# One decoder layer step on one core: last weight piece of each expert block in two halves, sample norm on ScalarE and GpSimd

## The reference

```python
logits = xt @ router_w + router_b            # 32 experts, top 4 of each token
# slots sorted by expert and padded into blocks of rows
def expert(args):
    xb, e = args
    gu = xb @ w_gu[e] + b_gu[e]              # (rows, 1024) @ (1024, 2048)
    gate, up = split(gu); gate = min(gate, 7); up = clip(up, -7, 7)
    act = (up + 1.0) * gate * sigmoid(1.702 * gate)
    return act @ w_down[e] + b_down[e]       # (rows, 1024) @ (1024, 1024)
x = layer_norm(ALPHA * h + moe, ln2_g, ln2_b)
```

## Time and profile before

| what | us |
|---|---|
| median of three runs | 1507.08 |
| the profiled execution, device time | 1507.74 |
| its span in the trace | 1506.0 |
| last weight piece needed by TensorE | 1488.2 |
| last VectorE operation starts | about 1502.7 |

### The profile page before, as it was taken

One profiled execution on the slowest core, in us unless ns is written; L12 is line 12 of the kernel. 1 busy time (PEld: TensorE's weight loads), 2 busy tenths in 40 slices (PEclk: granted clock), 3 DMA queues, 4 the chain that ended last, 5 costly groups with the idle time before them and its releaser, 6 DMA issues.

```text
span 1506.0 us, 21874 instructions
## 1 busy us (share of the span) xinstructions
PE 1466.5 (97%) x8606; PEld 733.3 (49%) x8606; DVE 446.8 (30%) x918; ACT 344.6 (23%) x863; POOL 107.3 (7%) x95
## 2 busy tenths in 40 slices
PE   9999999999999999999999999999999999999997
PEld 7777776566777764333333333333333333333332
DVE  3653777867410137201101111111111101101113
ACT  1224215631110023211212112122112111211213
POOL 1002231010502401000000000000000000000000
PEclk9999999999999999999999999999999999999999
DMA  6346697546269777999999999999999999999996
GB/s 214 112 168 176 214 292 228 184 153 197 93 213 297 289 278 281 421 418 429 427 427 428 429 429 429 427 429 427 429 428 429 428 429 429 428 429 428 430 427 262
DMA packets 110574, 507.75 MB, mean 337 GB/s; under 512 B 12548, under 2 KB 49012, under 8 KB 85844
## 3 DMA queue, kind: packets, MB, share of 16 engines
q1 hardware_dynamic: 103840, 499.64, 83.0%
q10 hardware_dynamic: 6676, 7.29, 1.7%
HBM read 491.19 MB, written 15.72 MB: 337 GB/s over the span
## 4 chain that ended last, share of the span: by engine, by line
PE 67%; DMA 21%; DVE 3%; ACT 1%; issue 1%; DVEq 0%; SPq 0%; ACTq 0%
DMA wGU<-in_w_gu 21%; PE ps L2483 16%; PE ps L1944 12%; PE ps L2488 8%; PE ps L2251 4%; PE ps L2424 4%; PE ps L1960 3%; PE ps L2471 3%; PE ps L2475 3%; PE ps L2268 2%; PE ps L2389 2%; PE ps L2281 2%; PE ps L2405 1%; DVE up L1837 1%; DVE up L1836 1%; PE ps L2026 1%
## 5 line engine op out<-in xcount | busy, mean ns | idle before, releaser
L2483 PE MATMUL ps<-wGU,xe 128*64 128x512 f32 x1536 | 343.7, 595 | 15.6 <-DMA wGU<-in_w_gu 15.6
L2488 PE MATMUL ps<-wD,aT 128*64 128x512 f32 x1024 | 226.8, 595 | 0.0
L2483 PEld LDWEIGHTS ps<-wGU,xe 128*64 128x64 f32 x1536 | 108.5, 137 | 238.0 <-issue 211.3
L1944 PE MATMUL ps<-xT,ring 128*128 128x288 f32 (+1 forms) x848 | 180.7, 410 | 2.2 <-PEq L200 0.7
L1833 DVE TENSOR_SCALAR sg<-sg 128x512 f32<-128x512 f32 x32 | 13.7, 427 | 558.3 <-ACT sg L1276 558.3
L1944 PEld LDWEIGHTS ps<-xT,ring 128*128 128x128 f32 (+1 forms) x848 | 126.5, 172 | 46.3 <-issue 4.4
L2488 PEld LDWEIGHTS ps<-wD,aT 128*64 128x64 f32 x1024 | 71.4, 137 | 133.0 <-issue 126.2
L1276 ACT ACTIVATE sg<-ps 128x512 f32<-128x512 f32 x32 | 19.1, 598 | 487.3 <-PE ps L2471 487.3
L1225 ACT ACTIVATE xe<-ps,lnT 128x64 f32<-128x64 f32 x262 | 81.4, 422 | 1.2 <-PE ps L2398 1.2
L402 PE MATMUL ps<-xT,ring 128*128 128x288 f32 x320 | 78.1, 407 | 0.0
L1292 ACT COPY ysb<-ps 64x512 f32<-64x512 f32 x64 | 37.1, 580 | 155.3 <-PE ps L2488 154.5
(11 more groups left out here) (487 smaller groups left out, 1418.9 us busy)
## 6 DMA issues: line engine op xcount, KB each, us to landing
wGU<-in_w_gu SPq DMA_DIRECT2D x128, 2048.0 KB, 34.9
wD<-in_w_down SPq DMA_DIRECT2D x64, 2048.0 KB, 36.1
ring<-in_w_in SPq DMA_DIRECT2D x21, 2048.0 KB, 8.9
out<-hst SPq DMA_DIRECT2D x8, 1024.0 KB, 6.0
ringS<-in_ssd_proj SPq DMA_DIRECT2D x4, 2048.0 KB, 8.9
wbuf<-prompt_A_rows ACTq DMA_DIRECT2D x16, 384.0 KB, 4.3
out<-Sb SPq DMA_DIRECT2D x2, 2048.0 KB
ring<-in_hg_proj SPq DMA_DIRECT2D x2, 2048.0 KB, 9.2
```

The source lines that it names most:

```text
L1944: last = m.matmul(ps[h, b, 0:T], ring[c % 2][:, k, n * P + h.start:n * P + h.stop], xT[:, k, :], start=(k == 0), stop=(k == KD - 1))
L2483: last = m.matmul(ps[half[h], bank, :], xe[:, f, hx, :], wgu[n][:, k, col + CW * h:col + CW * h + CW], start=(i == 0 and k == 0), stop=False)
L2488: last = m.matmul(ps[half[h], B_Y, :], aT[:, k, i - 4, :], wdn[n][:, k, CW * h:CW * h + CW], start=False, stop=(i == 5 and k == 3))
```

## The change

Pieces 0 to 3 stay as they are. Piece 4 stays one transfer of 2 MB, but each partition now gets rows 2p and 2p+1 of each half of 256 rows: two runs of 8 KB. Piece 5 becomes two transfers of 1 MB, 256 rows each, with a semaphore of its own for the first half; TensorE waits for the first half before k = 0 and for the second before k = 2. The transposes of `up` take columns two apart in two halves, to match. In the tail the norm of the samples leaves VectorE: it only multiplies mean and 1/sigma (128 x 1), ScalarE makes x/sigma - mean/sigma in one operation, GpSimd multiplies by the weight and adds the bias, and ScalarE issues the output transfer. Some semaphores are merged to make room (`q_cb` into `q_A`, `h_ot` into `h_nt`, `t_gb` into `t_vt`); the merged waits are for the same events.

```diff
-                    rows = 256 if i < 4 else 512
-                    sp.dma_start(dst[:], src[0, bass.ds(e, 1), r:r + rows, :].rearrange("a (p k) n -> p (a k) n", p=P)).then_inc(sem, 16)
+                    if i < 4:
+                        sp.dma_start(dst[:], src[0, bass.ds(e, 1), r:r + 256, :].rearrange("a (p k) n -> p (a k) n", p=P)).then_inc(sem, 16)
+                        return
+                    if i == 4:
+                        sp.dma_start(dst[:].rearrange("p (s k) n -> p s k n", s=2),
+                                     src[0, bass.ds(e, 1), r:r + 512, :].rearrange("a (s p k) n -> p (a s) k n", s=2, p=P)).then_inc(sem, 16)
+                        return
+                    for s in range(2):
+                        sp.dma_start(dst[:, 2 * s:2 * s + 2, :], src[0, bass.ds(e, 1), r + 256 * s:r + 256 * s + 256, :]
+                                     .rearrange("a (p k) n -> p (a k) n", p=P)).then_inc(sem if s else m_h[odd], 16)
...
-                for n in range(5):
+                for n in range(4):
                     sp.wait_ge(f_y, n + 1)
-                    if n == 2:
-                        sp.dma_start(y_sample.rearrange("b s d -> (b s) d").rearrange("s (q c) -> q s c", q=4), yqo[:]).then_inc(s_out, 16)
-                        continue
...
+                pool.wait_ge(g_ln, 16 * 12)
+                pool.wait_ge(f_ys, 1)
+                g.tensor_tensor(yqo[:], yqo[:], lnw4[:], ALU.mult).then_inc(f_ys, 1)
+                pool.wait_ge(f_ys, 2)
+                g.tensor_tensor(yqo[:], yqo[:], lnb4[:], ALU.add).then_inc(f_ys, 1)
...
                 rooted(1)
+                act.wait_ge(f_r, 3)
+                a.activation(yqo[:], ps[:, B_YS, 0:256], ACT.Identity, scale=fvar[:, 2:3], bias=mu2[:, 2:3]).then_inc(f_ys, 1)
                 rooted(2)
+                act.wait_ge(f_ys, 3)
+                act.dma_start(y_sample.rearrange("b s d -> (b s) d").rearrange("s (q c) -> q s c", q=4), yqo[:]).then_inc(s_out, 16)
...
-                lstep(v.scalar_tensor_tensor(yqo[:], ps[:, B_YS, 0:256], mu2[:, 2:3], lnw4[:], ALU.add, ALU.mult))
...
-                v.scalar_tensor_tensor(yqo[:], yqo[:], fvar[:, 2:3], lnb4[:], ALU.mult, ALU.add).then_inc(f_y, 1)
+                v.tensor_tensor(mu2[:, 2:3], mu2[:, 2:3], fvar[:, 2:3], ALU.mult).then_inc(f_r, 1)
...
-                    src = up[:].rearrange("q (p k) -> q k p", k=4)
+                    src = up[:].rearrange("q (s p k) -> q s k p", s=2, k=2)
...
-                        pe.wait_ge(m_w[n], loaded)
+                        if i == 5:
+                            pe.wait_ge(m_h[1 if odd else 0], half_loaded)
+                        else:
+                            pe.wait_ge(m_w[n], loaded)
...
                             for k in range(4):
+                                if i == 5 and k == 2:
+                                    pe.wait_ge(m_w[n], loaded)
```

More of the change, by code:

```diff
@@ L527, in build @@
         q_dx = S("dta_by_batch_ready")
-        q_A = S("A_ready")
+        q_A = S("A_then_scores_ready")
         q_dif = S("decay_exponents_ready")
         q_exp = S("decays_ready")
-        q_cb = S("scores_ready")
         q_cm = S("scores_copied")
@@ L586, in build @@
         h_n = S("o_normalised")
-        h_nt = S("o_transposed")
+        h_nt = S("sample_then_prompt_o_transposed")
         h_nc = S("o_transposed_copied")
-        h_ot, h_os = S("sample_o_transposed"), S("sample_o_copied")
+        h_os = S("sample_o_copied")
         g_s, g_b = S("ssd_branch_ready"), S("ssd_branch_gated")
@@ L595, in build @@
         m_w = [S(f"expert_piece_loaded{i}") for i in range(RING + 1)]
+        m_h = [S(f"last_piece_half_loaded{i}") for i in range(2)]
         m_re, m_ok = S("first_experts_reloaded"), S("first_experts_right")
         t_wr, t_b3 = S("router_loaded"), S("expert_bias_parts_ready")
-        t_vt, t_gs, t_gb = S("ln_vectors_transposed"), S("router_weights_scaled"), S("router_offsets_ready")
+        t_vt, t_gs = S("ln_vectors_transposed_then_router_offsets_ready"), S("router_weights_scaled")
         nc.clear_and_free_semaphores(projecting)
@@ L622, in build @@
         f_n = S("sample_mean_ready")
-        f_c, f_v, f_r, f_q = S("ln2_last_mean_ready"), S("ln2_sums_ready"), S("ln2_variance_ready"), S("ln2_rooted")
+        f_c, f_v, f_r, f_q = S("ln2_last_mean_ready"), S("ln2_sums_ready"), S("ln2_variance_or_sample_shift_ready"), S("ln2_rooted")
         f_y = S("y_ready")
+        f_ys = S("sample_y_scaled_then_weighed_then_ready")
         lstep = Steps(S("last_dve_step"))
@@ L814, in _, with piece @@
                 ssd_weights(1)
-                def piece(e, i, n, sem):
+                def piece(e, i, n, sem, odd=0):
                     src, dst, r = (w_gu, wgu[n], 256 * i) if i < 4 else (w_down, wdn[n], 512 * (i - 4))
-                    rows = 256 if i < 4 else 512
-                    sp.dma_start(dst[:], src[0, bass.ds(e, 1), r:r + rows, :].rearrange("a (p k) n -> p (a k) n", p=P)).then_inc(sem, 16)
+                    if i < 4:
[8 more added lines that the diff above has]
+                                     .rearrange("a (p k) n -> p (a k) n", p=P)).then_inc(sem if s else m_h[odd], 16)
                 sp.wait_ge(s_out, 192)
@@ L885, in _ @@
                     sp.wait_ge(m_f, g - RING if g < 2 * RING + 1 else g - RING + 1)
-                    piece(e, g % 6, (g - 1) % RING, m_w[(g - 1) % RING])
+                    piece(e, g % 6, (g - 1) % RING, m_w[(g - 1) % RING], g // 6 % 2)
                 def reload(it, r):
@@ L893, in reload @@
                         sp.wait_ge(m_f, it * 36 + (g - RING + 1))
-                        piece(e, i, (g - 1) % RING, m_w[(g - 1) % RING])
+                        piece(e, i, (g - 1) % RING, m_w[(g - 1) % RING], r % 2)
                 end = last_block(sp)
@@ L904, in _ @@
                     sp.dma_start(lnb4[bands[q], :], ln2_b[0, 256 * q:256 * q + 256].partition_broadcast(32)).then_inc(g_ln, 16)
-                for n in range(5):
+                for n in range(4):
                     sp.wait_ge(f_y, n + 1)
-                    if n == 2:
-                        sp.dma_start(y_sample.rearrange("b s d -> (b s) d").rearrange("s (q c) -> q s c", q=4), yqo[:]).then_inc(s_out, 16)
-                        continue
-                    t, h = n // 3, n % 3
+                    t, h = n // 2, n % 2
                     cols = slice(CW * h, CW * h + CW)
@@ L1045, in _ @@
                 for g in range(SG):
-                    act.wait_ge(q_cb, g + 1)
+                    act.wait_ge(q_A, g + 2)
                     a.copy(cbm[:, g, 32:SC], ps[:, g, 32:SC])
@@ L1194, in _ @@
                         evacuate(I_GB + 4)
-                    act.wait_ge(h_nt, h + 1)
+                    act.wait_ge(h_nt, h + 2)
                     a.activation(onT[:, h, 0:SEQ], ps[:, h % 4, 0:SEQ], ACT.Copy, scale=hgw[:, h:h + 1]).then_inc(h_nc, 1)
@@ L1300, in rooted @@
                 def rooted(j):
-                    act.wait_ge(f_r, j + 1)
+                    act.wait_ge(f_r, (1, 2, 4)[j])
                     t = (0, 2, 1)[j]
@@ L1642, in _ @@
                     v.tensor_tensor(s, s, ps[:, 0:4, :].rearrange("p h (b v) -> p h b v", b=4), ALU.add).then_inc(h_sa, 1)
-                dve.wait_ge(h_ot, 1)
+                dve.wait_ge(h_nt, 1)
                 for c in range(2):
@@ L1663, in _ @@
                     v.tensor_tensor(mT[:, c, :], gB[:, c, :], tmpA[c % 2][:], ALU.add).then_inc(g_m, 1)
-                dve.wait_ge(t_gb, 1)
+                dve.wait_ge(t_vt, 2)
                 v.tensor_copy(gvec[:], ps[:, 3, 0:E_])
@@ L1983, in _ @@
                     m.matmul(ps[:, g, 32:T - P], b_[:, P:2 * P], c_[:, P:2 * P], start=True, stop=True)
-                    m.matmul(ps[0:32, g, 0:32], b_[:, 2 * P:T], c_[:, 2 * P:T], start=True, stop=True).then_inc(q_cb, 1)
+                    m.matmul(ps[0:32, g, 0:32], b_[:, 2 * P:T], c_[:, 2 * P:T], start=True, stop=True).then_inc(q_A, 1)
                 project(2)
@@ L2225, in _ @@
                     last = m.transpose(ps[:, 4, P * c:P * c + P], ots[:, c, :], ident[:])
-                last.then_inc(h_ot, 1)
+                last.then_inc(h_nt, 1)
                 project(I_GB + 2)
@@ L2271, in _ @@
                         pe.wait_ge(t_gs, 1)
-                        m.matmul(ps[:, 3, 0:2 * E_], ones[:], gsm[:].rearrange("p i e -> p (i e)"), start=True, stop=True).then_inc(t_gb, 1)
+                        m.matmul(ps[:, 3, 0:2 * E_], ones[:], gsm[:].rearrange("p i e -> p (i e)"), start=True, stop=True).then_inc(t_vt, 1)
                 def mix(j, ks=range(KD)):
@@ L2401, in turn_a @@
                 def turn_a():
-                    src = up[:].rearrange("q (p k) -> q k p", k=4)
+                    src = up[:].rearrange("q (s p k) -> q s k p", s=2, k=2)
                     for f in range(4):
-                        last = m.transpose(ps[:, B_AT, f * P:(f + 1) * P], src[:, f, :], ident[:])
```

(2 more changed lines are left out.)

## The result

The changed kernel takes 1514.44 us (median of 7 runs, 1513.78 to 1515.18) against 1507.77 us for the kernel before on the same chips (7 runs, 1506.42 to 1511.61): ratio 1.0042, interval 1.0032 to 1.0052. It is 6.7 us slower. I had forecast +2.7 us and a range that ended at 1511.6 us, so the prediction was wrong.

What follows compares the result with a forecast made beforehand. The prediction took the weight stream's DMA rate, about 429 GB/s, as the bound, followed by an 18 us tail. Its terms, 3.0 + 0.2 - 0.1 - 0.4 = +2.7 us on 1507.08, gave 1509.8 us, range 1506.2 to 1511.6.

Steps and rivals of the forecast that it cites:

- Part 4: Tail: VectorE loses two operations to ScalarE and GpSimd, samples' transfer not last; -0.4 us, bounds 0 and -0.9.
- Part 1: Weight stream: eight more packets per engine at 6.5 ns in each of 58 `w_down` pieces; +3.0 us.
- Part 2: Weight stream: one more transfer a block, 29 at 6.5 ns; +0.2 us, bounds 0 and 2 us.
- Part 3: TensorE: added waits hidden in steady work; in the last block piece 5's first half lands earlier; -0.1 us.
- The rival without a toll: Weight stream: 8 KB packets cost nothing extra, the tail's gain stands alone; 1506.6 us, chance 0.34.
- the one of long packets: Weight stream: 16 KB is past the best size, each `w_down` piece gains 72 ns; 1502.4 us, chance 0.05.
- the dearer toll: Weight stream: 8 KB runs read no better than 4 KB rows, or halves' ends cost more; 1512.6 us, chance 0.11.

Runs made afterwards that it cites:

- runs2: Kernel before with pieces 4 and 5 in eight runs of 2 KB per partition, 56 more packets per engine: 1538.74 us against 1508.07, ratio 1.0208.
- weights_only: Changed kernel without its tail: pieces 4 and 5 as changed, sample norm as in the kernel before; 1513.24 us against 1508.07, ratio 1.0030.
- runs8: Kernel before with pieces 4 and 5 each one transfer in two 8 KB runs per partition, no added transfer: 1513.04 us against 1508.07, ratio 1.0033.
- runs4: Kernel before with pieces 4 and 5 in four runs of 4 KB per partition, 24 more packets per engine: 1521.60 us against 1507.91, ratio 1.0089.

## Why the prediction was wrong

- **Part 4, the tail, -0.4 us, measured +1.9.** This step failed in sign. That VectorE's chain gets 0.4 us shorter up to L1897 was right (8.77 to 8.39 us behind the copy), though `weigh2(2)` itself hardly moved: it also waits for ScalarE's square (0.36 us of wait in the changed kernel's trace), a wait that I had overlooked. What failed are two sentences. "GpSimd's two operations at 0.73 us": costed as if alone, they cost GpSimd 0.3 us more and VectorE's last pair 0.6 us, which eats the gain: SP's last issue ends 11.98 us behind the copy, 11.77 before, which is 0.2 of the 1.9 us. And "so the samples' transfer is not last", which is the rest: I compared issue times, 0.6 us apart, and not landings. It was issued 0.5 us ahead of the prompt's last, but on four engines and beside the prompt's packets its last one is moved 4.1 us after the issue began (1508.62 to about 1512.7), the prompt's last 3.0 us after (1509.16 to about 1512.2), and it ended the kernel. The bound that I had set, 0 if ScalarE and GpSimd come out last, had no price for that case, as it left the transfer's own duration out.
- **Part 1, the packets, +3.0 us.** Mechanism right, the term mis-sized. A packet costs 9.4 ns and not 6.5: 464 x 9.4 ns = 4.4 us. The bound of 9.3 ns and +4.3 us was right. It came from the two shortest packet sizes, and I had put it aside as farthest from 8 KB. The stretches of short packets are 2 to 4 us long, and 1% of the 4 KB row is 1.6 ns already, so they could not fix the few ns that remain; I should have kept the forecast nearer the middle of 5.4 to 9.3. The 3.5 ns and +1.6 us that this part quotes as another estimate are further off: runs2 would have lost 11 us.
- **Part 2**, the added transfers, 0.2 us: not resolved. The 37 us quoted there for 29 pairs of halves are refuted by weights_only, +5.2 us in all. The 72 ns of its bound rest on 4,893 ns a piece where 8 x 610.7 gives 4,886 ns, so 65 ns; the bound hardly moves. SP's longer issues held nothing up, as predicted: windows without gaps, and TensorE waits for no `wD` piece.
- **Part 3**, -0.1 us: gone. The wait for piece 5 vanished from the trace (before, weight loads ended seven waits with a `wD` piece, 2.8 us in all, after none), yet the 32 matmuls and the copy behind them take the same 7.13 us. A weight load that comes 0.27 us late was thus hidden.
- **The sum** with what was measured: 4.4 + 1.9 = 6.3 us, within the interval of the whole (4.8 to 7.8 us) and close to the 6.7 of the medians. The likeliest size was short by 4 us in all, 2.3 from part 4 and 1.4 from part 1; the remaining 0.3 is within the noise. The range failed by leaving part 4 one-sided: 9.3 ns together with the tail's true price was in none of my cases. The rival without a toll is refuted by runs8, the one of long packets by all of them, and the dearer toll by runs4, which was no dearer per packet. That last rival has a slip: 8 x 6.7 ns a piece makes 3.1 us for part 1 and 2.8 us for the sum, which passes 3.0 us from 7.1 ns on.

## What to carry to other kernels

Where transfers bound a stage without gaps, count the packets per engine: each added one cost 9.4 ns here (8.8 to 10.5), with runs of 8, 4 or 2 KB, so cutting 16 KB runs in two cost 1.5% of a piece's time, and an earlier half was worth nothing though the last block's weight load had waited 0.55 us for it. For a transfer near the end, compare landings and not issues, and look at its outermost dimension: four steps there meant four engines here. Work handed from VectorE to GpSimd beside VectorE operations with two SBUF inputs wasn't free for VectorE, 0.6 us on 1.4.

## What was unexpected

Transfers onto 64 of the 128 partitions, one pair of them in each block, made the whole kernel 29% slower (1937.9 against 1508.1 us): from 1000 to 1900 us 279 GB/s flowed on average in place of 429. TensorE had next to no work from 1102 to 1106 us (0.10 us), and from 1104 to 1110 us its granted clock was 0.50, the lower of its two levels (1.2 GHz); the kernel's mean was 0.926. And the toll per packet stood unchanged within its intervals from 2 KB to 8 KB runs.
